# Clearing two scratch buffers in HBM: by SP in 28 stores inside the dense layer's weight stream, in place of by POOL in three stores during the attention

## What is computed

```python
h = x
for layer in range(2):
    hn = rms_norm(h, attn_norm[layer])
    if layer == 0:
        h = h + mla(hn, ...)                       # 8 heads, causal, low-rank q and kv, rotary part
    else:
        h = h + multiscale_pool(hn, pool_w, pool_scale)
    hn = rms_norm(h, ffn_norm[layer])
    if layer == 0:
        h = h + (silu(hn @ w_gate) * (hn @ w_up)) @ w_down        # dense, 2688 hidden channels
    else:
        h = h + moe_swiglu(hn, router, w_gate, w_up, w_down)      # top 2 of 8 experts, 1344 hidden channels
return rms_norm(h, final_norm)
```

## Time and profile before

| | |
|---|---|
| median of 3 runs | 1182.1 us (1180.71 to 1182.85) |
| the profiled execution: time | 1184.12 us |
| its span in the trace | 1182.5 us |
| PE busy | 1103.1 us, 93% of the span |
| DVE busy | 385.7 us, 33% |
| ACT busy | 278.1 us, 24% |
| POOL busy | 57.1 us, 5% |
| data moved by DMA | 225.26 MB, 190 GB/s on average |
| mean granted TensorE clock | 0.98 of full |

### The profile page before, as it was taken

How to read it: one execution, slowest core, us unless ns; L and a number is a source line. 1 busy time by engine, 2 the same in 40 slices (tenths; PEclk the granted TensorE clock), 3 DMA queues, 4 the chain that set the end, 5 groups by cost and what they waited for, 6 DMA issues and landing times.

```text
span 1182.5 us, 19051 instructions
## 1 busy us (share of the span) xinstructions
PE 1103.1 (93%) x7414; PEld 1002.0 (85%) x7414; DVE 385.7 (33%) x703; ACT 278.1 (24%) x533; POOL 57.1 (5%) x99
## 2 busy tenths in 40 slices
PE   5999999799999999999997899999999999999980
PEld 4878877688888888888786799999999999999980
DVE  5586672354244442453564001010101010101015
ACT  5445552242224222232340001010101010101011
POOL 2210110000000000000002000000000000000002
PEclk9999999899999999999998999999999999999995
DMA  7027758434415144151203999999999999999996
GB/s 254 17 91 196 215 150 206 130 116 134 107 54 141 52 126 106 53 142 53 71 19 138 285 274 270 272 266 301 267 303 280 304 283 305 281 298 286 301 237 232
DMA packets 273230, 225.26 MB, mean 190 GB/s; under 512 B 29968, under 2 KB 246032, under 8 KB 273200
## 3 DMA queue, kind: packets, MB, share of 16 engines
q1 hardware_dynamic: 260192, 185.88, 56.2%
q0 software_dynamic: 11616, 36.32, 10.8%
q10 hardware_dynamic: 1392, 2.64, 0.6%
HBM read 198.43 MB, written 26.35 MB: 190 GB/s over the span
## 4 chain that ended last, share of the span: by engine, by line
PE 86%; DVE 6%; DMA 5%; ACT 1%; issue 1%; POOL 0%; DVEq 0%; SPq 0%; ACTq 0%; POOLq 0%
PE bank L1303 26%; PE bank L1317 14%; PE bank L905 13%; PE bank L907 13%; PE bank L906 13%; DMA scratch<-in_ffn_norm 2%; PE bank L1077 1%; PE bank L1364 1%; DMA stage_own<-in_moe_w_up 1%; PE bank L917 1%; PE bank L1281 1%; PE bank L1207 1%; PE bank L1057 1%; PE bank L1068 1%; PE bank L1292 1%
## 5 line engine op out<-in xcount | busy, mean ns | idle before, releaser
L1303 PE MATMUL bank<-scratch,stage_own 128*128 128x128 f32 (+1 forms) x2720 | 327.5, 278 | 8.4 <-DMA stage_own<-in_moe_w_gate 3.0
L1303 PEld LDWEIGHTS bank<-scratch,stage_own 128*128 128x128 f32 x2720 | 318.2, 191 | 10.5 <-DMA stage_own<-in_moe_w_gate 3.4
L1821 DVE TENSOR_TENSOR qr_now<-krT,bank 128x128 f32<-128x128 f32 (+1 forms) x80 | 23.4, 292 | 378.1 <-ACT krT L855 378.1
L1317 PE MATMUL bank<-qr_now,stage_own 128*128 128x128 f32 (+1 forms) x1152 | 143.5, 278 | 0.0
L1317 PEld LDWEIGHTS bank<-qr_now,stage_own 128*128 128x128 f32 x1152 | 137.3, 192 | 0.0
L905 PE MATMUL bank<-big_hi,w_lo 128*128 128x512 f32 (+2 forms) x352 | 134.4, 382 | 0.0
L907 PE MATMUL bank<-big_hi,w_hi 128*128 128x512 f32 (+2 forms) x352 | 134.3, 381 | 0.0
L906 PE MATMUL bank<-big_lo,w_hi 128*128 128x512 f32 (+2 forms) x352 | 134.2, 381 | 0.0
L855 ACT ACTIVATE krT<-bank 128x128 f32<-128x128 f32 (+1 forms) x80 | 22.5, 281 | 376.9 <-PE bank L1303 376.9
L1390 DVE TENSOR_TENSOR w_lo<-stage_own,w_hi 128x1024 fp32r<-128x1024 f32 (+1 forms) x91 | 105.4, 1203 | 14.0 <-ACT w_hi L608 13.9
L608 ACT CAST w_hi<-stage_own 128x1024 fp32r<-128x1024 f32 (+1 forms) x91 | 88.9, 1032 | 15.0 <-DMA stage_own<-in_mla_w_down 6.5
(11 more groups left out here) (243 smaller groups left out, 1146.5 us busy)
## 6 DMA issues: line engine op xcount, KB each, us to landing
stage_own<-in_moe_w_gate SPq DMA_DIRECT2D x82, 512.0 KB, 5.9
stage_own<-in_moe_w_up SPq DMA_DIRECT2D x82, 512.0 KB, 6.3
stage_own<-in_moe_w_down SPq DMA_DIRECT2D x72, 512.0 KB, 4.6
stage_own<-in_ffn_w_gate SPq DMA_DIRECT2D x21, 512.0 KB, 5.7
stage_own<-in_ffn_w_up SPq DMA_DIRECT2D x21, 512.0 KB, 6.9
stage_own<-in_ffn_w_down SPq DMA_DIRECT2D x21, 512.0 KB, 3.6
xbuf<-zeros POOLq DMA_DIRECT2D x2, 5184.0 KB, 41.9
scratch<-xbuf POOLq DMA_DIRECT2D x9, 576.0 KB, 6.3
```

Of the source, the lines that this page charges most:

```text
L1303: last = t_.matmul(dst[:, 0:n], w[:, k * P:(k + 1) * P], xT[:, k, 0:n], start=k == 0, stop=k == KD - 1)
L1317: last = t_.matmul(bank[4 + k // 3][:, col:col + n], w[0:parts, k * P:(k + 1) * P], e_act[0:parts, par, 0:n], start=first and k % 3 == 0, ...
L1821: v.tensor_tensor(e_act[:, par, 0:n], e_silu[:, par, 0:n], bank[2 * par + 1][:, 0:n], ALU.mult).then_inc(prod_ready, 1)
```

## The change

The three stores of POOL go. A row of zeros of 1024 columns (`zero_rows`, the first 1024 columns of `scratch`) is written by POOL once PE has transposed the last normed rows of the dense layer's norm (`xnT_done` at 8), and SP stores the zeros inside its loop over the dense layer's weights: in each of the 7 turns one store of 166 rows into `ybuf` (from 83 partitions, each read twice) behind the six gate and up loads, and one of 124 rows into `xbuf` (from 124 partitions) behind each of the three w_down loads. SP waits for the zeros ahead of the first of them, ACT waits for all 28 stores before it writes to `scratch` again (the norm behind the dense layer), and POOL's wait before the scatter counts 28 stores in place of three. `xbuf` has 2604 rows now.

```diff
-XROWS = (JMAX + 2) * C
+XZERO = -(-(JMAX + 2) * C // (FI * FG))
+XROWS = FI * FG * XZERO
+YZERO = 2 * -(-(JMAX - E) * C // (2 * FI))
...
+        zero_rows = scratch[:, 0:D]
...
+        zeros_ready = sem("zeros_ready")
...
                 for j in range(FG):
                     for q, w in enumerate((f_gate, f_up)):
                         load("ffn", 2 * j + q, lambda st: [(cols(st, 8, P), w[:, :, bass.ds(i * (FG * P) + j * P, P)])], i)
+                sp.wait_ge(zeros_ready, 1)
+                sp.dma_start(ybuf[bass.ds(i * YZERO + (JMAX * C - FI * YZERO), YZERO), :].rearrange("(p r) n -> p r n", r=2),
+                             zero_rows[0:YZERO // 2, :].unsqueeze(1).broadcast_to([YZERO // 2, 2, D])).then_inc(zero_stored, 16)
                 for j in range(FG):
                     load("ffn", 2 * FG + j,
                          lambda st: [(st, a["ffn_w_down"][0, bass.ds(i * (FG * P) + j * P, P), :])], i)
+                    sp.dma_start(xbuf[bass.ds(i * (FG * XZERO) + j * XZERO, XZERO), :], zero_rows[0:XZERO, :]
+                                 ).then_inc(zero_stored, 16)
...
-            pool.wait_ge(weight_lo, plan.unit("pair", 1, 1) + 1)
-            half = (JMAX + 2) // 2 * C
-            for rows in (xbuf[0:half, :], xbuf[half:, :], ybuf[E * C:, :]):
-                pool.dma_start(rows.rearrange("(p r) (c n) -> p (r c) n", p=ZP, n=P),
-                               zeros[0:ZP, :].unsqueeze(1).broadcast_to([ZP, rows.shape[0] // ZP * (D // P), P])
-                               ).then_inc(zero_stored, 16)
...
+            pool.wait_ge(xnT_done, 2 * T)
+            g.memset(zero_rows, 0.0).then_inc(zeros_ready, 1)
             pool.wait_ge(xn_ready, 3 * T)
...
-            pool.wait_ge(zero_stored, 48)
+            pool.wait_ge(zero_stored, 16 * 4 * FI)
...
             ffn(FI - 1, last_splits)
 
 
+            act.wait_ge(zero_stored, 16 * 4 * FI)
             for t in range(T):
```

## The result

The changed kernel takes 1217.9 us (median of 4 runs, 1217.0 to 1219.5) against 1181.4 for the kernel before (1180.7 to 1182.9): a ratio of 1.0303, 95% interval 1.0279 to 1.0326, so 36 us slower. The forecast was slower as well, by 80. The profiled execution took 1217.35 us for a span of 1215.8; the traces stand 33.3 us apart, because the profiled execution of before lay 2.7 us above its median.

A forecast was written before the change was run, and what follows sets the result against it. PE was taken as the bound, losing time where POOL's zero stores delay it. The terms -13.5 + 18.3 + 6 x 12.15 + 2 = +79.7 us, added to the 1182.1 us median, gave 1262 us; range 1215 to 1315.

The forecast's parts named there:

- lower bound of 1228: Whole kernel: if weight shares move at 24.4 GB/s once other engines are idle, a turn is 55.6 us: +46, 1228 us.
- Gain, 13.5 us: Attention's end and dense layer's start: removing POOL's three zero stores and their descriptor writing saves 13.5 us together.
- the four pieces: Savings around the dense layer's start: DVE not held 2.3 us, x early 2.4, gain row early 5.98, upper PE clock 2.9.
- Cheap adds, nothing: Dense layer: POOL's memset (estimate 1 us), SP's wait for zeros, and ACT's and POOL's waits for 28 stores cost nothing.
- The cut into 4 and 1: Stores on SP's queue: 124 partitions go in 4 shares of 31, 83 partitions in one undivided share on one engine.
- the rival of 1168.6 us: Dense layer stores spread over all engines and hidden in each turn, leaving only the 13.5 us gain: 1168.6 us, chance 0.10.
- The first turn, 18.3 us: Dense layer's first turn: w_down loads land late behind the ybuf store, so PE waits 18.3 us for the activation.
- The turn, 61.1 us: Dense loop: the engine shared by all stores needs 61.1 us against 48.95, adding 12.15 us in each of six turns.
- the weights' share: Dense loop turn: nine weight loads take 0.36 x 48.95 = 17.6 us on the engine shared by all stores.
- The last turn, 2 us: Dense layer's last turn: PE's restart at the lower clock isn't hidden behind the ring there and costs 2 us.
- Partly spread rival, 1173 us: Dense layer: ybuf store cut in 2 or more, only the first turn late by some 4 us: 1173 us, chance 0.04.
- The signs to look for: Profile after: no gain-row wait or 3.5 us tensor_scalar, slow w_down loads, ybuf landings about 28 us, seven dips, 61 us turns.

The follow-up runs named there:

- the second run with an added POOL store: Best kernel (128- and 192-row stores, 1164.9 us) plus a POOL store of 9216 64-byte pieces, issued behind the 25th exponentials: 1170.4 us, ratio 0.9907 to the kernel before.

## Where the prediction was right, and which step failed

The direction and the mechanism were right, and the size was wrong: +79.7 us forecast, 36.5 measured between the medians and 33.3 between the traces. The step that failed is the length of a turn. The measured 1217.9 us is also below the forecast's own lower bound of 1228. It lies in the stated range of 1215 to 1315 only by the margin that was added for other reasons, and that is luck.

- **Gain, 13.5 us.** 14.1 measured. Each of the four pieces (DVE's hold, x, the gain row, the clock) is gone from its place. The two runs with an added POOL store show the first to be descriptor writing; the other three were not tested one by one.
- **Cheap adds, nothing.** The memset took 0.97 us for an estimate of 1. SP stood waiting for it and issued the first store right behind it, at 231.87 us; with even shapes nothing of these adds is left on PE's path.
- **The cut into 4 and 1.** Right, by the count of endings, and it decided the sign: with shapes of 16 or 14 shares the same change gains 16 to 17 us, where the rival of 1168.6 us had a gain of 13.5.
- **The first turn, 18.3 us.** 17.4 measured.
- **The turn, 61.1 us.** This is the step that failed: 53.9 measured, so 4.98 us in each of six turns and not 12.15. That is 43 us of the 46 by which the forecast of +79.7 missed the traces' +33.3. The mechanism held: the turn is the work of the engine that all stores share. Its three terms were too large. By the fit, the ybuf store is 166 x 0.155 = 25.7 us (27.9 forecast), the three xbuf shares are 14.4 (15.6) and the weights' share is 13.4, not 17.6. The ybuf term rests on the stretch with one engine at work, at 27 GB/s and not 24.4. How the rest divides is less sure: at the 23 GB/s of four engines the xbuf shares would be 16.5 us and the weights' 11.7.
- **Why the weights' share was too large.** It was a share of busy time, read where 16 engines work side by side, and such a share takes in packets that were slow among the others. The packets of the two traces fit this. In the turn of the earlier trace rows, 384 packets of 512 bytes an engine at a mean of 0.0325 us and 24 of 4 KB at 0.214 make the 17.6 us. At the medians of the changed kernel's turn, 0.027 and 0.159, the same packets would be 14.2 us. The text had 12.1 us as its lower bound, near what was measured, and took the share. What PE loses is the turn less 48.95 us, so 7.2 us of 61 (12%) made a term of 73 us into one of 30.
- **The last turn, 2 us.** 4.1 measured.
- **Partly spread rival, 1173 us.** It was forecast for the ybuf store in two; that run gave 1175.3.
- **The signs to look for.** No gain-row wait, dips in seven turns, w_down loads of 20.5 us (3.6 before), longer turns, and the part behind the dense layer unchanged but for 2.7 us: these are there. Turns of about 61 us are not, and the profile has no landing time for the ybuf stores. The text had named the lone engine's rate as what is mis-sized if turns are longer by less than 12 us; by the fit it was in part that, in larger part the weights' share.

## What to carry to other kernels

Before a store joins a hardware queue, look at its partitions. In every store counted here (1, 2, 4, 5, 14 and 16 shares) the largest number up to 16 that divides the partitions of both sides was the number of engines that carried it; 128, 96 or 84 partitions were cheap where 127 and 83 weren't. Loads of such shapes were not tried. Count the endings in the queue's packets to see it. Where one engine's work makes a loop's turn, the loss is a difference of two large numbers, so measure both in the stretch that they come from, and say how an error of a tenth in one moves it.

## What the runs showed of the hardware that was not expected

- A queue with a few-share DMA holds its issuer, not only the DMAs behind: 15 us for SP at a w_down load, 20 to 30 us for ACT at three stores.
- An engine's rate depends on its company: 27 GB/s alone, 23 for each of four, 20.8 for each of five, for stores of 4 KB rows. Five shares were slower than four, for the whole kernel by 6 us.
- While POOL writes descriptors (3.9 us for 9216 pieces), a DVE tensor_scalar of 0.35 us takes 3.18; while the same store's data move, it takes 0.35.
- PE's halt of 2.6 us in the second run with an added POOL store cost over 4: the clock behind a wait can cost more than half as much again.
